# Expert gate and up projections in blocks of 512 inner columns instead of 256

## The reference

```python
for e in range(8):
    y = y + gate[:, e:e + 1] * (silu(x @ wg[e]) * (x @ wu[e])) @ wd[e]
```

## Time and profile before

| what | value |
|---|---|
| median of 3 runs | 1352.4 us |
| profiled execution: span from first to last instruction | 1350.1 us |
| PE busy | 1262.2 us, 93% |
| DVE busy | 1046.8 us, 78% |
| ACT busy | 802.5 us, 59% |
| loads of expert weights | 264 of 1 MB |

### The profile page before, as it was taken

One profiled execution on the slowest core, in us unless ns is written; L12 is line 12 of the kernel. 1 busy time (PEld: TensorE's weight loads), 2 busy tenths in 40 slices (PEclk: granted clock), 3 DMA queues, 4 the chain that ended last, 5 costly groups with the idle time before them and its releaser, 6 DMA issues.

```text
span 1350.1 us, 22286 instructions
## 1 busy us (share of the span) xinstructions
PE 1262.2 (93%) x8696; PEld 1174.4 (87%) x8696; DVE 1046.8 (78%) x1016; ACT 802.5 (59%) x901; POOL 56.5 (4%) x34
## 2 busy tenths in 40 slices
PE   6999999989875989999999999999999999999993
PEld 4899999979874869999998998998998998998992
DVE  6734343469998668889889889888888888888886
ACT  3533333354653456766776766776776776776771
POOL 0000000001642000000000000000000000000000
PEclk9999999999887989999999999999999999999997
DMA  9854444253030407998998998998998998998931
GB/s 276 266 172 157 159 158 150 60 158 105 13 121 32 156 32 237 370 358 284 370 361 277 367 363 278 366 363 275 367 363 279 366 350 292 365 366 282 366 140 37
DMA packets 249538, 332.66 MB, mean 246 GB/s; under 512 B 6404, under 2 KB 222820, under 8 KB 249450
## 3 DMA queue, kind: packets, MB, share of 16 engines
q1 hardware_dynamic: 249283, 331.28, 73.2%
q10 hardware_dynamic: 199, 0.62, 0.2%
HBM read 330.44 MB, written 2.84 MB: 247 GB/s over the span
## 4 chain that ended last, share of the span: by engine, by line
PE 80%; DVE 14%; ACT 3%; issue 2%; DMA 1%; DVEq 0%; ACTq 0%
PE bank L1068 35%; PE bank L1088 18%; PE bank L889 15%; PE bank L918 6%; DVE cacc L1321 5%; PE bank L1032 2%; PE bank L1077 1%; PE bank L838 1%; DVE w_lo L1165 1%; PE bank L1053 1%; ACT w_hi L543 1%; DVE acc L1469 1%; DMA spool<-in_state_pool_dram 1%; PE bank L874 1%; DVE uc_lo L1349 1%
## 5 line engine op out<-in xcount | busy, mean ns | idle before, releaser
L1165 DVE TENSOR_TENSOR w_lo<-raw,w_hi 128x2048 fp32r<-128x2048 f32 x309 | 707.9, 2292 | 200.7 <-ACT w_hi L543 200.1
L543 ACT CAST w_hi<-raw 128x2048 fp32r<-128x2048 f32 x309 | 590.9, 1913 | 260.2 <-PE bank L889 107.6
L1068 PE MATMUL bank<-w_hi,xg_hi 128*128 128x256 f32 x1408 | 401.6, 285 | 5.3 <-DVE acc L1469 3.6
L1068 PE MATMUL bank<-w_hi,xg_lo 128*128 128x256 f32 x1408 | 394.0, 280 | 0.0
L1068 PE MATMUL bank<-w_lo,xg_hi 128*128 128x256 f32 x1408 | 393.9, 280 | 0.0
L1068 PEld LDWEIGHTS bank<-w_hi,xg_hi 128*128 128x128 f32 x1408 | 265.4, 189 | 13.2 <-issue 8.9
L1068 PEld LDWEIGHTS bank<-w_lo,xg_hi 128*128 128x128 f32 x1408 | 266.0, 189 | 3.2
L1068 PEld LDWEIGHTS bank<-w_hi,xg_lo 128*128 128x128 f32 x1408 | 265.2, 188 | 0.0
L889 PE MATMUL bank<-x_hi,w_hi 128*128 128x304 f32 (+1 forms) x544 | 166.2, 305 | 8.5 <-DVE x_lo L1252 5.3
L889 PE MATMUL bank<-x_hi,w_lo 128*128 128x304 f32 (+1 forms) x544 | 164.3, 302 | 0.0
L889 PE MATMUL bank<-x_lo,w_hi 128*128 128x304 f32 (+1 forms) x544 | 163.6, 301 | 0.0
(11 more groups left out here) (191 smaller groups left out, 1337.8 us busy)
## 6 DMA issues: line engine op xcount, KB each, us to landing
raw<-in_moe_w_gate_dram SPq DMA_DIRECT2D x88, 1024.0 KB, 5.6
raw<-in_moe_w_up_dram SPq DMA_DIRECT2D x88, 1024.0 KB, 5.9
raw<-in_moe_w_down_dram SPq DMA_DIRECT2D x88, 1024.0 KB, 5.2
raw<-in_conv_w_dram SPq DMA_DIRECT2D x12, 1024.0 KB, 5.4
raw<-in_ffn_w_gate_dram SPq DMA_DIRECT2D x11, 1024.0 KB, 8.0
raw<-in_ffn_w_up_dram SPq DMA_DIRECT2D x11, 1024.0 KB, 8.1
raw<-in_ffn_w_down_dram SPq DMA_DIRECT2D x11, 1024.0 KB, 4.9
poolw<-in_pool_w_dram SPq DMA_DIRECT2D x1, 1024.0 KB, 11.1
```

The lines of the kernel that those rows point to most:

```text
L543: act.copy(w_hi[t % SPLIT][:], raw[t % RAW][:]).then_inc(hi_ready, 1)
L1068: last = pe.matmul(bank[:, 0:TW], x[:, c, :], w[:, c, :], start=(c == 0 and k == 0), stop=(c == KC - 1 and k == 2))
L1165: dve.tensor_tensor(w_lo[t % SPLIT][:], raw[t % RAW][:], w_hi[t % SPLIT][:], ALU.subtract).then_inc(split_ready, 1)
```

## The change

A block is now `BW = 512` inner columns. 2816 columns make five blocks of 512 and one of 256, `NB = 6`. A gate or up tile of a wide block holds half of the input rows (512 rows x 512 columns, rows of 2 KB in memory), so a block has two gate tiles, two up tiles and two down tiles; the last block has one of each, in the old shape. An expert still has 33 tiles of 1 MB. A wide tile is used by 4 chunks x 3 = 12 matmuls of 512 columns. Activation, product, turn (four transposes) and the halves of the turned block cover 512 columns at once. The order of a block on PE is gate, gate, turn of the block before, up, up, down, down of the block before; at the end of an expert it is gate, turn, up, gather, down, down, turn, gathered turn, down. The lists of ACT and DVE are rewritten for it. The buffers `hn`, `sgn`, `ht_hi` and `ht_lo` double; `g_row` and `b_row` move to the memory of `xg_hi` and `xg_lo`, and so their loads wait for the last product. The banks of the scatter change with the banks of gate and up.

```diff
-        hn = area("hn", [P, TW], F32, M1 + 8192)
+        hn = area("hn", [P, BW], F32, M1 + 8192)
-        g_row = area("g_row", [P, D], F32, M1 + 13440)
+        g_row = area("g_row", [P, D], F32, M1)
...
+        FIRST = [0] + [6 * b - 2 for b in range(1, NB)]
+        def halves(b):
+            return 2 if b < NB - 1 else 1
...
-        SCATTER_BANKS = (1, 4, 5, 3, 6, 7)
+        SCATTER_BANKS = (0, 4, 5, 2, 6, 7)
...
+                b = max(k for k in range(NB) if FIRST[k] <= j)
+                at_tile = j - FIRST[b]
+                if at_tile < 2 * halves(b):
+                    w = (moe_w_gate, moe_w_up)[at_tile // halves(b)]
+                    if b == NB - 1:
+                        src, r0, rows, view = w, 0, D, wide
+                    else:
+                        src, r0, rows, view = w, at_tile % 2 * HALF, HALF, quad
+                    cols = slice(b * BW, min((b + 1) * BW, F))
...
-            sp.wait_ge(acc_ready, 6)
-            sp.dma_start(g_row[:], ...)
+            sp.wait_ge(h_done, FC + E * NB)
+            sp.dma_start(g_row[:], ...)
...
 ACT, one expert
                 hi(T_MOE + 3, n)
-                silu(0, 0)
-                for j in range(1, NJ):
-                    g = 3 * j - 1
-                    hi(T_MOE + g + 2, n)
-                    turn_evac(j - 1)
...
-                    hi(T_MOE + g + 3, n)
-                    silu(j, g)
-                    if not last or j < NJ - 1:
-                        hi(T_MOE + g + 4, n)
-                if not last:
-                    rows_evac(n + 1)
-                turn_evac(NJ - 1)
-                if not last:
-                    xg_evac(n + 1)
-                    hi(T_MOE + TE + 1, n)
-                    hi(T_MOE + TE + 2, n)
+                hi(T_MOE + 4, n)
+                silu(0)
+                hi(T_MOE + 5, n)
+                for j in range(1, NB):
+                    g = T_MOE + FIRST[j]
+                    hi(g + 2, n)
+                    if j < NB - 1:
+                        hi(g + 3, n)
+                        hi(g + 4, n)
+                        turn_evac(j - 1)
...
+                        silu(j)
+                        hi(g + 5, n)
+                        hi(g + 6, n)
+                        hi(g + 7, n)
+                    else:
+                        turn_evac(j - 1)
+                        hi(g + 3, n)
+                        silu(j)
+                        hi(g + 4, n)
+                        if not last:
+                            hi(g + 5, n)
+                            rows_evac(n + 1)
+                        turn_evac(j)
+                        if not last:
+                            hi(g + 6, n)
+                            xg_evac(n + 1)
+                            hi(g + 7, n)
...
 PE
-                    for c in range(KC):
-                        for k, (x, w) in enumerate(((xg_hi, wh), (xg_hi, wl), (xg_lo, wh))):
-                            last = pe.matmul(bank[:, 0:TW], x[:, c, :], w[:, c, :], ...)
+                    for half in range(halves(j)):
...
+                        for c in range(chunks):
+                            f = half * chunks + c
+                            for k, (x, m) in enumerate(((xg_hi, wh), (xg_hi, wl), (xg_lo, wh))):
+                                done = pe.matmul(bank[:, 0:w], x[:, f, :], m[:, c, :], ...)
...
 DVE, one expert
                 lo(T_MOE + 3, n)
-                mult(0, 1)
+                lo(T_MOE + 4, n)
+                lo(T_MOE + 5, n)
+                mult(0)
                 add_scattered(e, r * SCAT + e * 6, range(4))
...
+                for j in range(1, NB):
+                    g = T_MOE + FIRST[j]
+                    lo(g + 2, n)
...
+                    if j < NB - 1:
+                        lo(g + 3, n)
+                        lo(g + 4, n)
+                        turn_low(j - 1)
+                        lo(g + 5, n)
+                        lo(g + 6, n)
+                        mult(j)
+                        lo(g + 7, n)
...
+                    else:
+                        turn_low(j - 1)
+                        lo(g + 3, n)
+                        lo(g + 4, n)
+                        mult(j)
+                        if not last:
+                            lo(g + 5, n)
+                        turn_low(j)
+                        if not last:
+                            lo(g + 6, n)
+                            xg_low(n + 1)
+                            lo(g + 7, n)
```

More of the change, by code:

```diff
@@ L76, in build_trunk @@
     TE = 3 * NJ
+    NB = NJ // 2 + 1
+    BW = 2 * TW
     assert TE % RAW == 0 and TE % SPLIT == 0
@@ L305, in tall, with quad, gate_end, up_end @@
             return t[:, :].rearrange("p (k f) -> p k f", k=TR)
+        def quad(t):
+            return t[:, :].rearrange("p (k f) -> p k f", k=KC // 2)
+        FIRST = [0] + [6 * b - 2 for b in range(1, NB)]
+        def halves(b):
+            return 2 if b < NB - 1 else 1
+        def gate_end(b):
+            return FIRST[b] + halves(b) - 1
+        def up_end(b):
+            return FIRST[b] + 2 * halves(b) - 1
         pext_s = pext[:, :, PCTX + NPR:PEXT].rearrange("p c (b j) -> p c b j", b=SB)
@@ L409, in expert_tile @@
             def expert_tile(e, j):
[L411 to L422, removed]
+                b = max(k for k in range(NB) if FIRST[k] <= j)
[7 more added lines that the diff above has]
+                    cols = slice(b * BW, min((b + 1) * BW, F))
+                    return src[0, bass.ds(e, 1), r0:r0 + rows, cols].rearrange("o (c p) f -> p (o c) f", p=P), view
+                i = 2 * (b - 1) + at_tile - 2 * halves(b)
+                src = moe_w_down[0].rearrange("e (j r) f -> (e j) r f", r=TW)[bass.ds(e * NJ + i, 1)]
+                return src.rearrange("o (c p) f -> p (o c) f", p=P), tall
             def load_expert(n, e, j):
@@ L746, in one_expert, with silu @@
                 t0 = n * TE
[L748 to L751, removed]
+                def silu(j):
+                    w = halves(j) * TW
+                    act.wait_ge(tile_used, t0 + (T_MOE + gate_end(j) + 1))
+                    act.wait_ge(h_done, n * NB + (FC + j))
+                    act.activation(sgn[:, 0:w], ps[(j + 1) % 2][:, 0:w], ACT.Silu).then_inc(silu_done, 1)
@@ L753, in turn_evac @@
                 def turn_evac(j):
-                    act.wait_ge(h_turned, n * NJ + (j + 1))
-                    act.copy(ht_hi[:], ps[4 + j % 2][:, 0:TR * P].rearrange("p (c n) -> p c n", c=TR))\
+                    k = halves(j) * TR
+                    act.wait_ge(h_turned, n * NB + (j + 1))
+                    act.copy(ht_hi[:, 0:k, :], ps[4 + j % 2][:, 0:k * P].rearrange("p (c n) -> p c n", c=k))\
                         .then_inc(ht_hi_done, 1)
                 hi(T_MOE + 3, n)
-                silu(0, 0)
@@ L773, in one_expert @@
[L773 to L777 removed]
+                hi(T_MOE + 4, n)
[8 more added lines that the diff above has]
+                        turn_evac(j - 1)
+                        if j == 1:
+                            act.wait_ge(sel_turned, n + 1)
+                            act.copy(sel_t[:], ps[5][:, 0:NM]).then_inc(sel_t_done, 1)
+                        silu(j)
[15 more added lines that the diff above has]
+                            hi(g + 7, n)
@@ L1060, in one_expert, with rows_block @@
                 scattered = r * SCAT + e * 6
-                def rows_block(bank, j, t):
-                    pe.wait_ge(split_ready, n * TE + (t + 1))
-                    wh, wl = wide(w_hi[t % SPLIT]), wide(w_lo[t % SPLIT])
-                    for c in range(KC):
-                        for k, (x, w) in enumerate(((xg_hi, wh), (xg_hi, wl), (xg_lo, wh))):
-                            last = pe.matmul(bank[:, 0:TW], x[:, c, :], w[:, c, :],
-                                             start=(c == 0 and k == 0), stop=(c == KC - 1 and k == 2))
-                    last.then_inc(tile_used, 1)
+                def rows_block(bank, j, g):
+                    w = halves(j) * TW
+                    for half in range(halves(j)):
+                        t = T_MOE + g + half
+                        pe.wait_ge(split_ready, n * TE + (t + 1))
+                        view, chunks = (quad, KC // 2) if halves(j) == 2 else (wide, KC)
+                        wh, wl = view(w_hi[t % SPLIT]), view(w_lo[t % SPLIT])
+                        for c in range(chunks):
+                            f = half * chunks + c
+                            for k, (x, m) in enumerate(((xg_hi, wh), (xg_hi, wl), (xg_lo, wh))):
+                                done = pe.matmul(bank[:, 0:w], x[:, f, :], m[:, c, :],
+                                                 start=(f == 0 and k == 0), stop=(f == KC - 1 and k == 2))
+                        done.then_inc(tile_used, 1)
@@ L1072, in turn_h @@
                 def turn_h(j):
-                    pe.wait_ge(h_done, n * NJ + (FC + j + 1))
+                    pe.wait_ge(h_done, n * NB + (FC + j + 1))
                     if j >= 2:
```

(65 more changed lines are left out.)

22 lines of the change are left out of this document (10 added, 12 removed).

## The result

Four runs of the changed kernel have a median of 1357.26 us (1357.01 to 1357.77), four of the kernel before 1351.87. The ratio is 1.0047, 95% interval 1.0032 to 1.0061: slower by 5.4 us, where 3.7 were forecast. The profiled execution took 1357.01 us, with a span of 1355.3 against 1350.1.

The account below looks back on a forecast made before the run. The prediction took PE to bound the expert stage, not the weight loads. Losing 14.1 us at seven expert ends and saving 10.4 elsewhere gave +3.7: span 1353.8, plus 2.3 for the runs' median, 1356.1 us, range 1350.5 to 1363.

Parts of the forecast that it names:

- What bounds: Expert stage: PE bounds it, 33 tiles at 2.8 us being 92 of 102.89 us; weight loads wait for ring slots.
- Wide tile 2.75 us, block 16.94: Gate and up tiles on PE: 2.75 us instead of 2.83; a block of six tiles 16.94 us instead of 17.26.
- Inside a block no stall: ACT and DVE beside PE within a block: they keep up, cost zero, with 0.9 us of cover.
- Ends, 2.0 us each: Seven expert ends: stalls before gathered turn (0.18), last down tile (0.59) and next expert (1.24), 14.1 us lost in all.
- The rest of an expert, 1.39 us saved: Expert outside its end: 85.82 us instead of 87.21; over eight experts 11.1, less 0.7 for the first, 10.4 us saved.
- Rows of the last norm: Last norm's two row loads, now waiting for the last product: there by 1328, wanted at 1339.80, so hidden.
- Sum: Whole kernel: 14.1 us lost minus 10.4 saved gives +3.7 us, median 1356.1 us.
- (a): Rival, wide gate matmuls closer together than 229 ns: at 223 ns 11.5 us less, 1344.6; chance 0.09.
- (d): Rival, wide matmuls without any surplus, 213 ns each: 30.7 us less, 1325.4; chance 0.03.
- (b): Rival, no difference: part of the end stalls (0.18 and 0.59) doesn't appear, 5.4 us less, 1350.7; chance 0.20.
- (c): Rival, much slower: clock falls at expert ends, 1.6 us each, 1367, or 1362 at half of them; chance 0.13.

Follow-up runs that it names:

- the rows of 2 KB: Kernel before, its gate and up loads (except the last block's) fetching half the input rows x 512 columns, matmuls unchanged: 1350.91 us, ratio 0.9996.
- The swap of xg: Changed kernel with the split of the gathered rows ahead of the cast of the next expert's second tile, on ACT and DVE: 1347.56 us, ratio 0.9976.
- the turns between the down tiles: Changed kernel with last block's and gathered rows' turns between the previous block's down tiles, copies ahead of casts: 1339.55 us, ratio 0.9908.
- one of 2.0 in the old order: Kernel before with the next expert's second tile cast and halved ahead of the split of the gathered rows: 1371.07 us, ratio 1.0148.

## Why the prediction was right

- **What bounds (part 1 of the text):** right. PE; the loads don't count, shown by the rows of 2 KB.
- **Wide tile 2.75 us, block 16.94:** right to 0.01 us. The Trainium skill (TensorE: Matmul & The Clock Gate, "Wait — 56ns, not 53.3ns?") gives 215.7 ns for 512 columns; no tile of any run here has that pace, and 229 ns is the mean in all of them.
- **Inside a block no stall:** right.
- **Ends, 2.0 us each:** right in place and order. From the last gate tile's end to the next expert is 17.86 us, forecast 17.70. The swap of xg alone takes back 1.5 an end, the turns between the down tiles 2.6 in all. So the stalls are 2.6, not 2.0, and an end without them is 15.4 us, not 15.68. Of the 0.6 more, 0.3 is the hidden wait, which the walk counted as work of the gathered turn. The last down tile waits for ht_lo in either case, so this error left the sum as it was. The rest is 0.16 by which the next expert comes later than in the walk, and 0.1 that its first tiles lose behind the stall.
- **The rest of an expert, 1.39 us saved:** right in size (103.53 - 17.86 = 85.67, forecast 85.82), but the source given for it was off. The text put the saving down to the narrow tiles' surplus, 0.08 a tile; against narrow matmuls in the same order the width gives 0.80 to 0.83. The other 0.7 comes with the order. The scatter's stall of 0.5 for 0.7 is a part of it, and narrow tiles that run at the fast pace more often in the new order, some 0.25, are another; what is left wasn't separated.
- **Luck:** the end was forecast 0.16 too short and the rest of an expert 0.15 too long. The two cancel, and the period came out at 103.53 for 103.52.
- **Rows of the last norm:** loads issued at 1324.79, first use at 1345.00 without a wait: hidden.
- **Sum:** +3.7 forecast, +4.2 from the first expert on. The other 1.0 of the span's 5.2 lies ahead of it, in code that is the same.
- **Rivals:** (a) and (d), closer matmuls: none in any run. (b), stalls that don't appear: they all did. (c), the clock: it didn't fall in this kernel, at stalls of 0.7 and 1.2 us; but at one of 2.0 in the old order it fell five times in seven. No run shows where between them the limit lies, or that the length of the stall alone decides: the same 2.0 us left the clock alone twice, and ahead of the first expert the clock fell behind 1.0 us without matmuls, after a run of small ones.

Open: what switches a 256-column matmul between 113 and 118 ns. The load traffic alone doesn't do it (in the kernel before, 509 to 511, they start 118 ns apart with no load under way), nor the granted clock (1.00 at both paces), nor a stall ahead (both paces occur with and without one).

## What to carry to other kernels

When PE is full and every engine has a written order, look at what each list does while it waits: an operation that is ready but stands behind one that isn't is late by that wait, and if PE needs it the time is lost. One swap (9 us here) can be worth more than the change of shape (6 us) that brought in the need for it. A wider moving operand pays by the surplus of the narrow form in the trace, not by the number of instructions it removes. Measure what a stage would take without stalls before trusting the length of a row in it: the gathered turn looked like 1.08 us of work and was 0.8.

## What the runs showed of the hardware

In these runs matmuls of 256 columns have two paces, 113 and 118 ns, that hold for whole tiles, at a granted clock of 1.00; those of 512 columns have one, 229 ns. A stall of PE of 2.0 us, with matmuls dense before and behind it, lowered the clock behind five of seven ends and not behind the other two. Stalls of 0.7 and 1.2 us, three microseconds apart, did so at none of seven ends.
